# FFN down products two tiles behind, normed sums through PSUM, weight casts in other places: a two-block transformer kernel

## The chip, the cores and the metric

The kernel runs on one core of one Trainium2 chip. Its metric is the device time of one execution in microseconds. Five engines work side by side, each through its own queue in order: TensorE (PE, with its weight loads PEld), VectorE (DVE), ScalarE (ACT), GpSimd (POOL), and SyncE (SP), which here only issues DMAs. They wait for each other through semaphores.

## What is computed

The input is one sequence of 256 tokens of width 1024. Two transformer blocks follow each other. Cut to what matters:

```
first_block:  x = layer_norm(a*x + 0.5*swiglu(x))        # FFN0: silu(x@Wg) * (x@Wu) @ Wd, inner width 2816
              x = layer_norm(a*x + hybrid_mixer(x))      # q/k/v, three kinds of attention, gates, w_out
              x = layer_norm(a*x + 0.5*swiglu(x))        # FFN1
second_block: u = rmsnorm(h) @ w_in ...                  # convolution, gated delta rule, sparse attention
              h = h + rmsnorm(mixed @ w_o, w)            # normed sum 3
              f = causal_dwconv(rmsnorm(h) @ w_up) + b   # FFN2: three taps over the tokens
              h = h + rmsnorm((gelu(f_gate)*f_val) @ w_down, w)   # normed sum 4
              e = (p @ w_ple) * sigmoid(h @ w_ple_gate)
              h = h + rmsnorm(e, w)
```

All is float32. A product of float32 matrices is made of three TensorE passes over operands that are split into a high and a low part.

## The kernel before

**The stream.** All weights lie in one stream in the order of their use, as chunks of eight blocks of 128x128 (512 KB). SP loads chunk n into slot n % 4 of `ring`. ACT casts it to the high part (`high`, L1165, semaphore `hi_ready`), POOL subtracts for the low part in two instructions of 128x512 (L498, `lo_ready`), and TensorE takes both (`mm`, L529). When TensorE starts on a chunk it raises `used`; the cast of chunk n waits until chunk n-3 has been started, and stands in ACT's queue like all else, so what is behind it waits too. `feed_to` and `feed` (L1167 to L1177) issue the casts up to a given chunk; where they are called decides where the casts stand in ACT's order.

**An FFN** (`ffn`, L690) has 22 tiles of 128 hidden features. `gate_up_first` makes tiles 0 and 1 together from chunks 0 to 3, into `acc`, which is free then. `gate_up(f)` makes gate and up of tile f, 16 blocks (two chunks) and 48 matmuls of 256 columns, into a PSUM bank. ACT applies SiLU (`ffn_act`, L1183) and DVE multiplies and splits the result into `hT` (`hidden`, L1641; semaphores `h_made`, `hidden`). In FFN2 `geglu_act` (L1200) and `conv_hidden` do the same with a tap on ACT, four taps on DVE (L1672), GELU (L1213), product (L1680) and split. `down(f)` multiplies tile f by 8 blocks (one chunk, 12 matmuls of 512 columns) and adds into the four banks of `acc`. `down(0)` overwrites `acc`, so it waits for `h_made` of both first tiles. The order is: tiles 0 and 1, gate_up(2), down(0), down(1), gate_up(3), down(2), gate_up(4), down(3), and so on, gate_up(20), gate_up(21), and the last three down products in pieces (`HELD`). `ffn_end(f)` is the block up to which `feed` counts before ACT works on tile f. `hT` has four slots; `hidden(f)` waits until down(f-4) is done.

**Between the parts** there is a norm. For the layer norms `layer_half` (L1705) adds x and acc; `turn` transposes the normed tokens on TensorE (L651) into four PSUM banks, two of the eight xT tiles in each, ACT writes `xT_high` from them (L1255 to L1265) and DVE `xT_low` (L1848 to L1868). `layer_out` (L1734, L1735) then makes the residual from res and rows, a product and a sum of 128x1024 for each of two halves of the tokens (called tokens 0 and 1 below); it stands behind the q/k turn at once, and in FFN1 between the hidden tiles.

**Normed sums 3 and 4** (`add_normed`, L1787) stand before FFN2 and behind it. ACT squares each half row of `acc` (`acc_rms`, L1403) and takes the root (L1233); DVE multiplies acc by the norm's weights into `xs` (L1793, `acc_read`) and then multiplies by the reciprocal and adds the old x (L1797). Behind sum 3, ACT squares the sum again (`x_rms`) and copies the four `ple` banks (`ple_copy`, L1590), whose banks the turn before FFN2 writes. The last part, `into_acc`, is x @ w_ple_gate in eight steps of one chunk.

## Time and profile before

| what | value |
|---|---|
| median of three executions | 1193.85 us (1192.21 to 1196.79) |
| profiled execution | 1193.65 us, span 1191.8 us |
| mean granted TensorE clock | 0.976 |
| TensorE busy | 1114.9 us, 94% |
| POOL busy | 908.9 us, 76% |
| ACT busy | 628.6 us, 53% |
| DVE busy | 516.9 us, 43% |
| DMA | 193.40 MB, 162 GB/s |

The span runs from the first to the last instruction, and all times in the trace count from its start. FFN0 lies at 10 to 188 us, the q/k tiles at 200, FFN1 at 463 to 648, FFN2 at 963 to 1148, the last product at 1157 to 1180. A window's row gives its length, then the busy time of PE, PEld, DVE, ACT and POOL with the number of instructions in brackets, then the granted clock, the busy share of the DMA engines and GB/s. A timeline's row gives start, length, engine, line, operation, output <- inputs, size and count, and in brackets how long the engine had been idle and who released it. "issue" there means that the profile shows no releaser. Matmul ends are modelled; the distance between starts tells the pace. The granted clock has 1.00 for 2.4 GHz and 0.50 for 1.2 GHz.

### The profile page before, as it was taken

Reading aid. Unit: us, or ns where it says so; the run is one execution under the profiler, and the core shown is the slowest. Engines: PE = TensorE matmul, PEld = TensorE weight load, DVE = VectorE, ACT = ScalarE, POOL = GpSimd, SP = SyncE. Lnnn points to the kernel's source line nnn. Section 1 sums busy time; section 2 is a strip of 40 time slices with the busy share of each in tenths; the row PEclk is TensorE's granted clock in tenths of the full one; section 3 lists DMA queues with packets and bytes.
Section 4 is the critical chain, followed back from the end, with each engine's and each line's share of the span. In section 5 each row is a group of like instructions: output and inputs, shape, how many; then the busy total and the mean of one; then the engine's idle time right before and its main releaser. Section 6 shows DMA issues by size and latency. Waiting matters only on the chain.

```text
span 1191.8 us, 22559 instructions
## 1 busy us (share of the span) xinstructions
PE 1114.9 (94%) x8040; PEld 1034.4 (87%) x8040; DVE 516.9 (43%) x979; ACT 628.6 (53%) x1012; POOL 908.9 (76%) x700
## 2 busy tenths in 40 slices
PE   6999998899999998899998899899899989999986
PEld 6999998898988897799998889899788879999964
DVE  3333116232336544511113547774665245455664
ACT  4444446555556755344444765554556575555553
POOL 7999995998553595999998599393225869999973
PEclk9999999999998999999999899999989999999988
DMA  7866664576331364566565366252213655666641
GB/s 253 323 203 199 194 192 127 175 207 189 112 114 54 107 200 160 171 194 191 188 194 186 106 201 188 89 159 72 71 54 118 192 159 178 193 190 187 196 151 53
DMA packets 52631, 193.40 MB, mean 162 GB/s; under 512 B 5840, under 2 KB 6096, under 8 KB 51920
## 3 DMA queue, kind: packets, MB, share of 16 engines
q1 hardware_dynamic: 50976, 184.57, 49.8%
q10 hardware_dynamic: 1584, 7.81, 1.8%
q8 instruction: 53, 0.87, 0.3%
q14 instruction: 18, 0.15, 0.0%
HBM read 191.31 MB, written 1.05 MB: 161 GB/s over the span
## 4 chain that ended last, share of the span: by engine, by line
POOL 51%; issue 31%; PE 14%; DVE 2%; POOLq 1%; ACT 1%; DVEq 0%; ACTq 0%
POOL weights_low L498 51%; PE banks L529 8%; PE acc L529 6%; POOLq L501 0%; DVE xs L1797 0%; POOLq L495 0%; DVE stat L1812 0%; DVE res L1810 0%; DVE res L1824 0%; DVE act_buf L1672 0%; DVE xs L1830 0%; DVE xs L1793 0%; ACT weights_high L1165 0%; DVE hf L1680 0%; ACT act_buf L1208 0%
## 5 line engine op out<-in xcount | busy, mean ns | idle before, releaser
L498 POOL TENSOR_TENSOR weights_low<-ring,weights_high 128x512 fp32r<-128x512 f32 x696 | 908.7, 1336 | 263.9 <-ACT weights_high L1165 260.7
L1165 ACT CAST weights_high<-ring 128x1024 fp32r<-128x1024 f32 x348 | 361.5, 1048 | 242.8 <-PE banks L529 123.7
L529 PE MATMUL banks<-xT_high,weights_high 128*128 128x256 f32 x1536 | 432.0, 281 | 3.3 <-POOL weights_low L498 2.8
L529 PE MATMUL banks<-xT_low,weights_high 128*128 128x256 f32 x1536 | 427.4, 278 | 0.0
L529 PE MATMUL banks<-xT_high,weights_low 128*128 128x256 f32 x1536 | 427.2, 278 | 0.0
L529 PEld LDWEIGHTS banks<-xT_high,weights_high 128*128 128x128 f32 x1536 | 290.7, 189 | 7.2 <-issue 3.0
L529 PEld LDWEIGHTS banks<-xT_low,weights_high 128*128 128x128 f32 x1536 | 290.9, 189 | 2.3
L529 PEld LDWEIGHTS banks<-xT_high,weights_low 128*128 128x128 f32 x1536 | 290.3, 189 | 0.0
L1647 DVE TENSOR_TENSOR hf<-act_buf,banks 128x256 f32<-128x256 f32 x40 | 16.9, 421 | 247.4 <-ACT act_buf L1191 247.3
L529 PE MATMUL acc<-weights_high,hT_high 128*128 128x512 f32 x264 | 103.6, 392 | 7.6 <-issue 6.7
L529 PE MATMUL acc<-weights_low,hT_high 128*128 128x512 f32 x264 | 104.0, 394 | 0.0
L529 PE MATMUL acc<-weights_high,hT_low 128*128 128x512 f32 x264 | 103.0, 396 | 0.0
L529 PEld LDWEIGHTS acc<-weights_high,hT_high 128*128 128x128 f32 x264 | 50.0, 189 | 17.5 <-issue 7.7
L1672 DVE SCALAR_TENSOR_TENSOR act_buf<-banks,col,act_buf 128x255 f32<-128x255 f32 (+1 forms) x80 | 35.0, 478 | 58.9 <-ACT act_buf L1208 56.4
L529 PEld LDWEIGHTS acc<-weights_high,hT_low 128*128 128x128 f32 x264 | 49.9, 189 | 10.1
L1656 DVE TENSOR_TENSOR hT_low<-hf,hT_high 128x256 fp32r<-128x256 f32 x66 | 57.6, 873 | 2.3
L529 PEld LDWEIGHTS acc<-weights_low,hT_high 128*128 128x128 f32 x264 | 49.9, 189 | 9.2
L1279 ACT ACTIVATE prob<-sS,nmx 128x128 f32<-128x128 f32 x68 | 30.4, 448 | 48.1 <-DVE nmx L1886 47.9
L529 PE MATMUL acc<-xT_high,weights_high 128*128 128x256 f32 x144 | 39.0, 306 | 11.8 <-POOL weights_low L498 11.7
L1883 DVE SCALAR_TENSOR_TENSOR sS<-cst,banks 128x384 f32<-128x384 f32 x34 | 18.8, 554 | 64.5 <-issue 52.8
L1191 ACT ACTIVATE act_buf<-banks 128x256 f32<-128x256 f32 x40 | 15.4, 384 | 56.8 <-PE banks L529 56.8
L529 PEld LDWEIGHTS acc<-xT_high,weights_high 128*128 128x128 f32 x144 | 30.9, 214 | 12.2 <-issue 12.1
(337 smaller groups left out, 1620.6 us busy)
## 6 DMA issues: line engine op xcount, KB each, us to landing
ring<-in_stream SPq DMA_DIRECT2D x348, 512.0 KB, 3.6
rows<-in_big_rows ACTq DMA_DIRECT2D x3, 1024.0 KB, 6.9
rows<-in_big_rows ACTq DMA_DIRECT2D x3, 512.0 KB, 4.4
cst<-in_consts ACTq DMA_DIRECT2D x1, 1411.0 KB, 10.8
gates<-in_x_fm SPq DMA_DIRECT2D x2, 512.0 KB, 5.2
xs<-in_x_tm ACTq DMA_DIRECT2D x1, 1024.0 KB, 6.0
out<-xs SPq DMA_DIRECT2D x4, 256.0 KB, 2.1
pT<-in_p_fm ACTq DMA_DIRECT2D x1, 256.0 KB, 3.5
```

Source lines behind the costliest of these rows:

```text
L498: last = nc.gpsimd.tensor_tensor(wlo[:, slot, hs], ring[:, slot, hs], whi[:, slot, hs].bitcast(F32), ALU.subtract)
L529: ins = nc.tensor.matmul(o, lhsT, rhs, start=start, stop=stop, **kw)
L1165: nc.scalar.copy(whi[:, ch % RING, :], ring[:, ch % RING, :]).then_inc(S["hi_ready"], 1)
L1191: nc.scalar.activation(act_buf[:, f % 2, 0:T], ffn_tile(n, f, it)[:, 0:T], ACT.Silu).then_inc(S["act_done"], 1)
L1279: nc.scalar.activation(prob[:, j % 2, lo:hi], sS[:, j % 2, lo:hi], ACT.Exp, bias=nmx[:, j % 2, t:t + 1], accum_out=den[:, j % 2, t:t + 1]) ...
L1647: v.tensor_tensor(hf[:, f % 2, :], act_buf[:, f % 2, 0:T], ffn_tile(n, f, it)[:, T:2 * T], ALU.mult).then_inc(S["h_made"], 1)
L1656: v.tensor_tensor(hT[1][:, f % GROUP, :], hf[:, f % 2, :], hT[0][:, f % GROUP, :].bitcast(F32), ALU.subtract).then_inc(S["hidden"], 1)
L1672: last = v.scalar_tensor_tensor(buf, ffn_tile(2, f, it)[:, half * T:half * T + T - sh], conv_col(3 * (half * NF + f) + tap, it), buf, ALU. ...
L1883: mark(v.scalar_tensor_tensor(sS[:, j % 2, :], c("negdist"), slope, bank(f"s{j}")[:, 0:384], ALU.mult, ALU.add), "biased", j + 1)
```

## The change

The FFNs run two gate_up tiles ahead of the down products instead of one, and the stream is packed in that order: tiles 0 and 1, gate_up(2), gate_up(3), down(0), down(1), gate_up(4), down(2), gate_up(5), down(3) and so on to gate_up(20), down(18), gate_up(21), and the last three as before. `ffn_end` follows. ACT's `turn` casts the following part's fourth chunk between the xT tiles of its second and third bank. In `add_normed` the product with the weights stays in `acc`, the sum reads it from there, and DVE waits for each of its own instructions; TensorE's next use of `acc` waits for the sums (`norm_sum` 8, `xn_ready` 11) where it waited for the products (`acc_read` 16 and 20). Two casts around sum 3 and those of the last part stand behind squares that they stood before.

```
 def ffn_end(f):
-    return 32 if f < 2 else 24 * f + (8 if f < NF - 1 else 0)
+    return 32 if f < 2 else 16 * f + 16 if f < 4 else 24 * f
...
-            def into_acc(src, each, first_wait):
+            def into_acc(src, each, free):
...
-                        pe.wait_ge(S["acc_read"], first_wait)
+                        pe.wait_ge(S[free[0]], free[1])
...
-                    need(pe, "acc_read", 4 * n_acc_before)
+                    if first_acc:
+                        pe.wait_ge(S[first_acc[0]], first_acc[1])
...
-                    at[0] = b0 + (32 if f == 2 else 24 * f - 8 if f < NF - 1 else 24 * f - 16)
+                    at[0] = b0 + (16 * f if f < 4 else 24 * f - 16)
...
-                    at[0] = b0 + (48 if very_first else 24 * f + 32)
+                    at[0] = b0 + (64 + 8 * f if isinstance(it, int) and f < 2 else 24 * f + 48)
...
-                n_acc_before = (0, 2, 4)[n]
+                first_acc = (None, ("acc_read", 8), ("norm_sum", 8))[n]
                 gate_up_first()
                 gate_up(2)
+                gate_up(3)
                 down(0)
                 down(1)
-                for f in range(3, 1 + GROUP):
-                    gate_up(f)
-                    down(f - 1)
+                gate_up(4)
+                down(2)
                 with nc.tensor.Fori(1, (NF - 2) // GROUP - 1) as it:
                     for f in range(1, 1 + GROUP):
                         gate_up(f + GROUP, it - 1)
-                        down(f - 1 + GROUP, it - 1)
+                        down(f - 2 + GROUP, it - 1)
                 for f in range(NF - 1 - GROUP, NF - 1):
                     gate_up(f)
-                    if f < NF - 2:
-                        down(f - 1)
+                    down(f - 2)
                 gate_up(NF - 1)
...
-            into_acc(xT, (("xT_high", 32), ("xT_ready", 32)), 20)
+            into_acc(xT, (("xT_high", 32), ("xT_ready", 32)), ("xn_ready", 11))
...
-            def turn(i, gain=None, bias=None):
+            def turn(i, following, gain=None, bias=None):
                 for g in range(4):
+                    if g == 2:
+                        feed_to(PART_AT[following] // CB + 4)
...
             acc_rms(12, 0)
-            feed_to(PART_AT["ple"] // CB + 3)
+            feed_to(PART_AT["ple"] // CB + 2)
             acc_rms(12, 1)
             x_rms(4, 0, 0)
+            feed_to(PART_AT["ffn2"] // CB + 1)
...
             acc_rms(16, 0)
-            feed_to(PART_AT["ple_gate"] // CB + 1)
             acc_rms(16, 1)
-            feed_to(PART_AT["ple_gate"] // CB + 3)
-            turn(4)
+            feed_to(PART_AT["ple_gate"] // CB + 2)
+            turn(4, "ple_gate")
...
-                        mark(v.tensor_tensor(xs[:, dst, tok, hs], acc[:, 2 * tok + half, :], rows[:, i % 2, hs], ALU.mult),
-                             "acc_read", (12, 16)[i - 3] + 2 * tok + half + 1)
+                        link(v.tensor_tensor(acc[:, 2 * tok + half, :], acc[:, 2 * tok + half, :], rows[:, i % 2, hs], ALU.mult))
                     link(recip(stds + tok + 1, tok))
                     for half, (_, hs) in enumerate(halves(tok)):
-                        v.scalar_tensor_tensor(xs[:, dst, tok, hs], xs[:, dst, tok, hs], stat[:, 6 + tok:7 + tok], xs[:, src, tok, hs],
-                                               ALU.mult, ALU.add).then_inc(S[sem], 1)
+                        mark(v.scalar_tensor_tensor(xs[:, dst, tok, hs], acc[:, 2 * tok + half, :], stat[:, 6 + tok:7 + tok],
+                                                    xs[:, src, tok, hs], ALU.mult, ALU.add), sem, sem0 + 2 * tok + half + 1)
...
-    parts = [by_k(np.concatenate([g[0], u[0], g[1], u[1]]), 4), g[2], u[2], d[0], d[1]]
-    for f in range(3, NF):
-        parts += [g[f], u[f]] + ([d[f - 1]] if f < NF - 2 else [])
+    parts = [by_k(np.concatenate([g[0], u[0], g[1], u[1]]), 4), g[2], u[2], g[3], u[3], d[0], d[1]]
+    for f in range(4, NF):
+        parts += [g[f], u[f]] + ([d[f - 2]] if f < NF - 1 else [])
```

**Start of an FFN, TensorE.** FFN0, the end of gate_up(2) (banks<-xT) and what follows, first before and then after the change; the number ahead is the place in the queue.

```order
113 L529 MATMUL banks<-xT_high,weights_high 128x256
114 L529 MATMUL banks<-xT_low,weights_high 128x256
115 L529 MATMUL banks<-xT_high,weights_low 128x256
116 L529 MATMUL acc<-weights_high,hT_high 128x512
117 L529 MATMUL acc<-weights_low,hT_high 128x512
118 L529 MATMUL acc<-weights_high,hT_low 128x512
```

```order
113 L529 MATMUL banks<-xT_high,weights_high 128x256
114 L529 MATMUL banks<-xT_low,weights_high 128x256
115 L529 MATMUL banks<-xT_high,weights_low 128x256
116 L529 MATMUL banks<-xT_high,weights_high 128x256
117 L529 MATMUL banks<-xT_low,weights_high 128x256
118 L529 MATMUL banks<-xT_high,weights_low 128x256
```

Before, the down products (acc<-weights, hT) follow at place 116; after, 48 matmuls of gate_up(3) stand there first, and they follow at 164.

**Start of FFN2, ACT.** Taps of tiles 0 and 1 from acc (L1208), GELU (L1213), casts of chunks (L1165), then tile 2 from its bank; before and after.

```order
579 L1165 CAST weights_high<-ring 128x1024 x4
580 L1208 ACTIVATE act_buf<-acc,col 128x256 x2
581 L1213 ACT_TABLE_LOAD
582 L1213 ACTIVATE gel<-act_buf 128x256
583 L1208 ACTIVATE act_buf<-acc,col 128x256 x2
584 L1213 ACTIVATE gel<-act_buf 128x256
585 L1165 CAST weights_high<-ring 128x1024 x3
586 L1208 ACTIVATE act_buf<-banks,col 128x256 x2
587 L1213 ACTIVATE gel<-act_buf 128x256
588 L1165 CAST weights_high<-ring 128x1024 x3
```

```order
586 L1165 CAST weights_high<-ring 128x1024 x3
587 L1208 ACTIVATE act_buf<-acc,col 128x256 x2
588 L1213 ACT_TABLE_LOAD
589 L1213 ACTIVATE gel<-act_buf 128x256
590 L1208 ACTIVATE act_buf<-acc,col 128x256 x2
591 L1213 ACTIVATE gel<-act_buf 128x256
592 L1165 CAST weights_high<-ring 128x1024 x2
593 L1208 ACTIVATE act_buf<-banks,col 128x256 x2
594 L1213 ACTIVATE gel<-act_buf 128x256
595 L1165 CAST weights_high<-ring 128x1024 x2
```

The casts ahead of tile 0 are three instead of four, since one moved into the turn; behind the GELU of tile 1 stand two instead of three, and behind tile 2 two instead of three.

**Turn before the q/k tiles, ACT.** xT tiles from the banks, the bias part of each bank's second tile (tmp), casts, and the first q/k copies; before and after.

```order
75 L1259 ACTIVATE xT_high<-banks,col 128x256 x2
76 L1265 ACTIVATE tmp<-xT_high,col 128x256
77 L1259 ACTIVATE xT_high<-banks,col 128x256 x2
78 L1265 ACTIVATE tmp<-xT_high,col 128x256
79 L1259 ACTIVATE xT_high<-banks,col 128x256 x2
80 L1265 ACTIVATE tmp<-xT_high,col 128x256
81 L1165 CAST weights_high<-ring 128x1024 x3
82 L1328 ACTIVATE qkT<-acc 128x256 x3
```

```order
76 L1261 ACTIVATE xT_high<-banks,col 128x256 x2
77 L1267 ACTIVATE tmp<-xT_high,col 128x256
78 L1165 CAST weights_high<-ring 128x1024
79 L1261 ACTIVATE xT_high<-banks,col 128x256 x2
80 L1267 ACTIVATE tmp<-xT_high,col 128x256
81 L1261 ACTIVATE xT_high<-banks,col 128x256 x2
82 L1267 ACTIVATE tmp<-xT_high,col 128x256
83 L1165 CAST weights_high<-ring 128x1024 x2
84 L1330 ACTIVATE qkT<-acc 128x256 x3
```

One of the three casts behind the tiles now stands in their middle.

**Last norm, ACT.** Squares of acc (tmp, stat<-acc), small steps, the root (stat<-stat), casts, xT tiles; before and after.

```order
664 L1403 ACTIVATE tmp,stat<-acc 128x512
665 L1233 ACTIVATE stat<-stat 128x1
666 L1165 CAST weights_high<-ring 128x1024
667 L1403 ACTIVATE tmp,stat<-acc 128x512
668 L1407 ACTIVATE stat<-stat,cst 128x1
669 L1403 ACTIVATE tmp,stat<-acc 128x512
670 L1233 ACTIVATE stat<-stat 128x1
671 L1165 CAST weights_high<-ring 128x1024 x2
672 L1255 CAST xT_high<-banks 128x256 x8
673 L1165 CAST weights_high<-ring 128x1024 x5
```

```order
671 L1405 ACTIVATE tmp,stat<-acc 128x512
672 L1233 ACTIVATE stat<-stat 128x1
673 L1405 ACTIVATE tmp,stat<-acc 128x512
674 L1409 ACTIVATE stat<-stat,cst 128x1
675 L1405 ACTIVATE tmp,stat<-acc 128x512
676 L1233 ACTIVATE stat<-stat 128x1
677 L1165 CAST weights_high<-ring 128x1024 x2
678 L1257 CAST xT_high<-banks 128x256 x4
679 L1165 CAST weights_high<-ring 128x1024 x2
680 L1257 CAST xT_high<-banks 128x256 x4
681 L1165 CAST weights_high<-ring 128x1024 x4
```

The cast between the squares of the two tokens is gone; two casts stand ahead of the xT tiles and two among them.

## Rows read from the trace of the kernel before

**Rows 1.** Windows of the FFN bodies: length, busy us of each engine, TensorE's clock, DMA.

```profile
30.00:60.00 30.00, 30.00 (x208) 27.66 (x207) 9.98 (x13) 12.81 (x15) 27.87 (x22) 1.00 0.89 322
...
540.00:570.00 30.00, 30.00 (x217) 28.03 (x217) 4.57 (x12) 12.79 (x15) 28.08 (x22) 1.00 0.62 191
...
1050.00:1080.00 30.00, 30.00 (x217) 28.03 (x216) 15.52 (x26) 15.01 (x23) 28.71 (x23) 1.00 0.59 190
```

**Rows 2.** Chain of waits in FFN2: start, us, what.

```profile
1002.25 2.75 PE acc L529 x12
1005.00 5.47 PE banks L529 x48
```

**Rows 3.** Timeline of FFN1's start: start, us, what, [idle before <- releaser].

```profile
479.69 7.13 POOL L498 TENSOR_TENSOR weights_low<-ring,weights_high 128x512 fp32r<-128x512 f32 x4
...
481.21 2.28 DVE L1734 TENSOR_TENSOR xs<-res,rows 128x1024 f32<-128x1024 f32 x1
...
485.73 0.42 DVE L1647 TENSOR_TENSOR hf<-act_buf,acc 128x256 f32<-128x256 f32 x1
...
486.25 0.47 PE L529 MATMUL acc<-weights_high,hT_high 128*128 128x512 f32 x1 [4.63 <-issue]
...
486.81 1.05 ACT L1165 CAST weights_high<-ring 128x1024 fp32r<-128x1024 f32 x1 [6.42 <-PE acc L529]
...
498.88 0.39 PE L529 MATMUL acc<-weights_high,hT_high 128*128 128x512 f32 x1
```

**Rows 4.** Window behind the wait in FFN1, columns as in rows 1.

```profile
486.00:490.00 4.00, 3.75 (x10) 2.96 (x11) 3.90 (x5) 1.33 (x2) 2.88 (x3) 0.59 0.44 134
```

**Rows 5.** Timeline of the first q/k tiles, TensorE, POOL and DVE.

```profile
206.29 16.52 POOL L498 TENSOR_TENSOR weights_low<-ring,weights_high 128x512 fp32r<-128x512 f32 x10 [4.24 <-ACT weights_high L1165]
...
206.57 2.10 DVE L1734 TENSOR_TENSOR xs<-res,rows 128x1024 f32<-128x1024 f32 x1
...
209.94 0.36 PE L529 MATMUL banks<-xT_high,weights_high 128*128 128x256 f32 x1 [1.44 <-POOL weights_low L498]
...
214.39 0.36 PE L529 MATMUL banks<-xT_high,weights_high 128*128 128x256 f32 x1 [1.38 <-POOL weights_low L498]
```

**Rows 6.** Timeline of FFN2's start, ACT and TensorE.

```profile
981.68 2.93 ACT L1165 CAST weights_high<-ring 128x1024 fp32r<-128x1024 f32 x3
...
982.33 0.47 PE L529 MATMUL acc<-weights_high,hT_high 128*128 128x512 f32 x1 [2.05 <-issue]
...
985.58 0.47 PE L529 MATMUL acc<-weights_high,hT_high 128*128 128x512 f32 x1 [0.24 <-POOL weights_low L498]
```

**Rows 7.** Timeline of the turn before FFN1, ACT and TensorE.

```profile
468.52 2.01 ACT L1165 CAST weights_high<-ring 128x1024 fp32r<-128x1024 f32 x2
...
472.31 0.36 PE L529 MATMUL acc<-xT_high,weights_high 128*128 128x256 f32 x1 [1.47 <-POOL weights_low L498]
```

**Rows 8.** Timeline of FFN2's end, DVE and TensorE.

```profile
1142.52 1.57 DVE L1680 TENSOR_TENSOR hf<-gel,act_buf 128x256 f32<-128x256 f32 x1 [0.48 <-ACT gel L1213]
...
1144.56 0.47 PE L529 MATMUL acc<-weights_high,hT_high 128*128 128x512 f32 x1 [0.65 <-DVE hT_high L1654]
```

**Rows 9.** Two source lines of DVE: ns min/median/max, first and last start, forms.

```profile
L1797 DVE SCALAR_TENSOR_TENSOR xs<-xs,stat x8: 747/1093/1781, 949.7 to 1154.1; 128x512 f32<-128x512 f32 x8
...
L1705 DVE SCALAR_TENSOR_TENSOR res<-xs,acc x8: 686/687/690, 189.4 to 458.5; 128x512 f32<-128x512 f32 x8
```

**Rows 10.** Timeline of the last norm, ACT and DVE.

```profile
1148.02 1.03 ACT L1165 CAST weights_high<-ring 128x1024 fp32r<-128x1024 f32 x1
...
1152.80 3.03 DVE L1797 SCALAR_TENSOR_TENSOR xs<-xs,stat 128x512 f32<-128x512 f32 x2
```

**Rows 11.** Timeline of the norm before FFN2, ACT and TensorE.

```profile
950.19 2.00 ACT L1165 CAST weights_high<-ring 128x1024 fp32r<-128x1024 f32 x2 [1.14 <-PE acc L529]
...
959.06 1.05 ACT L1590 COPY gates<-banks 128x512 f32<-128x512 f32 x2
...
960.37 2.93 PE L651 MATMUL banks<-cst,res 128*128 128x128 f32 x16 [3.40 <-DVE res L1784]
```

More of the change, by code:

```diff
@@ L907, in _ @@
                 branch_b(n)
-            into_acc(mT1, (("merged_high", 0), ("merged", 0)), 4)
+            into_acc(mT1, (("merged_high", 0), ("merged", 0)), ("acc_read", 4))
             turn(1)
@@ L1124, in _ @@
                 done(mix_part(o, 1))
-            into_acc(mT2, (("merged_high", 8), ("mixed", 0)), 12)
+            into_acc(mT2, (("merged_high", 8), ("mixed", 0)), ("acc_read", 12))
             pe.wait_ge(S["p_split"], 1)
@@ L1319, in _ @@
             feed_to(PART_AT["qk"] // CB + 3)
-            turn(0, "ln_g0", "ln_b0")
+            turn(0, "qk", "ln_g0", "ln_b0")
             scale = {0: 0.125, 2: float(np.float32(32 ** -0.5)), 4: 0.125}
@@ L1392, in _ @@
             feed_to(PART_AT["ffn1"] // CB + 3)
-            turn(1, "ln_g1", "ln_b1")
+            turn(1, "ffn1", "ln_g1", "ln_b1")
             rows_in(2)
@@ L1450, in _ @@
             feed_to(PART_AT["conv"] // CB + 3)
-            turn(2, "mix_pre")
+            turn(2, "conv", "mix_pre")
             def conv_silu(t):
@@ L1602, in _ @@
             feed_to(PART_AT["ffn2"] // CB + 3)
-            turn(3, "ffn_pre")
+            turn(3, "ffn2", "ffn_pre")
             rows_in(5)
@@ L1785, in rms_scaled, with add_normed @@
                                     ).then_inc(S["xn_ready"], 1)
-            def add_normed(i, src, dst, sq, stds, sem):
+            def add_normed(i, src, dst, sq, stds, sem, sem0):
                 dve.wait_ge(S[f"big_rows_in{i % 2}"], 16 * (i // 2 + 1))
@@ L2260, in _ @@
             merged_low(mT2, 7, bank("mix7"), "mixed", 8)
-            add_normed(3, 1, 0, (4, 6), 8, "norm_sum")
+            add_normed(3, 1, 0, (4, 6), 8, "norm_sum", 4)
             rms_scaled(0, 10 + 1, 0)
@@ L2266, in _ @@
             steps[0] += NF
-            add_normed(4, 0, 1, (12, 14), 12, "xn_ready")
+            add_normed(4, 0, 1, (12, 14), 12, "xn_ready", 7)
             turn(4)
```

## The prediction

> **What bounds the kernel now.** I read the windows first, then the waits of TensorE, then the timeline around each wait. In the body of an FFN the reader is to see TensorE busy for 30.00 of 30 us, with POOL close behind at 28.08 (FFN1) and 28.71 (FFN2) [rows 1]; the chain of waits gives a tile's two halves, 2.75 us for a down product and 5.47 us for a gate/up pair, 8.22 us a tile [rows 2]. A tile uses three stream chunks, so **TensorE needs one chunk every 2.74 us whatever it computes from it**, and POOL makes one (two instructions of 28.08/22 = 1.28 us) in 2.55 us. Nothing that shifts work inside the loop can gain there: 66 tiles stay at 8.22 us. What can be won are the places where TensorE stands still, and the change touches six of them. I go by chunk number inside a part, from chunk 0, since the stream is repacked in the new order and chunk n is needed at the same distance before and after.
>
> **FFN1, first down product.** The first down product starts at 486.25 after 4.63 us of waiting [rows 3]. What it waits for stands above it: acc still holds tiles 0 and 1, and the product of tile 1 (DVE L1647) ends at 485.73 + 0.42, because DVE first multiplies token 0's rows of the layer norm (L1734, 2.28 us, and its partner). Then comes the price of the long stop: the granted clock is 0.59 from 486 to 490 [rows 4], the half level of 1.2 GHz for most of it. The third down product starts at 498.88 and is chunk 10; from 481.62, where the wait began and chunk 6 was due, four chunks at 2.74 us would reach it at 492.6. So 6.3 us stand between this and no stop. After the change gate_up(3) fills 5.47 us, to 487.1, and h_made is there at 486.2: the wait is gone. Next late is POOL. It made chunks 7 and 8 from 479.69 to 486.82, 3.56 us each beside DVE's products [rows 3], and then lay idle; now it goes on, and DVE's rows of token 1 meet it. At 3.5 us a chunk, chunk 11 is ready at 486.82 + 3 x 3.5 = 497.3 against a need at 495.3: 2.0 us are lost again, and 0.2 for restarts. **Term: 4.1 us**, bounds 1.6 (4.4 us a chunk, as between TensorE's two late starts in [rows 5]) and 6.3. The row is nearest to 3.5, since DVE also has casts and waits between.
>
> ACT's order has to allow it. Its casts for tile 2 stop at block 48 instead of 56, so the SiLU of tile 2 no longer stands behind a cast that waits 6.42 us for the first down product [rows 3]. The same bound 24f holds later, with the same distance to the end of gate_up(f) as 24f + 8 had: no effect per tile.
>
> **FFN2, first down product.** Here the wait is 2.05 us [rows 6], with no lowered clock. But the second down product, chunk 7, waited too, for POOL, till 985.58; its cast is the first of the three at 981.68, behind both GELUs. That cast does not move: ACT finishes GELU of tile 1 in both orders before it. Now chunk 7 is the second half of gate_up(3), due at 983.0, and stands till 985.5 as before. One wait takes the other's place. **Term: 0.1 us**, bounds -0.3 and 2.2.
>
> **FFN0** has no wait there: from 30 to 60 us TensorE is busy 30.00 of 30 us, at 322 GB/s [rows 1]. ACT now issues the norm's 1 MB table after the SiLU of tile 3 without waiting for three casts, some 5 us earlier, while the start's tables still load. At 322 GB/s 1 MB is 3.3 us of the queues; the ring holds four chunks, 11 us. Term 0, bounds -1 and 0.
>
> **A cast between xT tiles.** In the turn before FFN1 chunk 3 is cast at 468.52, when all eight tiles are done, and TensorE waits 1.47 us for its low part [rows 7]. After tile 3 the cast starts at about 465.6, and the low part is ready before TensorE's need at 470.8. Tiles 4 to 7 come 1.05 us later; tile 4 is then there at 467.2 and is first used at 468. **Term: 1.5 us**, bounds 0.4 (if that 1.05 shows) and 1.6. In the turn before the q/k tiles TensorE waits 1.44 and 1.38 us, and POOL works 16.52 us on five chunks [rows 5], slowed by DVE's row products from 206.57 on. With chunk 3 out of the way before these begin, chunk 4 is in time (211), but chunk 5 is made wholly beside them and is late by 1.4 us, where the two waits made 2.8. **Term: 1.4 us**, bounds 0.5 and 2.8. Before the convolution and before FFN2 no such wait exists; the tiles that slip by 1.05 us are needed more than 2 us later: 0. Before the last product the cast of chunk 3 waits till TensorE has begun chunk 0 with xT tile 0; it stands before tiles 4 to 7 only, due 11 us later: 0.
>
> **End of FFN2.** The last tile's hidden product took 1.57 us beside POOL, and the last held unit waited 0.65 us for its cast [rows 8]. Before, gate_up(20) and gate_up(21) stood in a row; now a down product parts them, ACT's casts come sooner, and POOL is done earlier. **Term: 0.7 us**, bounds 0 and 0.8.
>
> **Normed sums through PSUM.** L1797 reads xs twice from SBUF and takes 0.747 to 1.781 us; L1705, the same operation and size with one input in acc, takes 0.686 to 0.690 [rows 9]. After the change the sum has one input in acc. In the last norm the pair for token 1 takes 3.03 us and ends at 1155.83, which releases the last transposes [rows 10]. Two at 0.69 save 1.6. The cast of 1.03 us that stood between the squares of tokens 0 and 1 moves behind them: 0.9 of it arrives, as DVE's rest becomes shorter too. Some 0.4 goes back since the transposes of the first half now end later than the second half's data. The in-place product is priced as L1705 too; the added waits of DVE for its own sums queue nothing but the next sum. The last product now waits for the sums instead of the first products, but xT waits for these sums anyway: 0. **Term: 2.1 us**, bounds 1.0 and 2.6. In the norm before FFN2 the transposes at 960.37 start just when ACT ends its copies of the ple banks (959.06 + 1.05) [rows 11], since they write those banks. ACT does the same work between 950.19 and that point, in another order, without a pause: two casts, six squares, four copies. **Term: 0**, bounds -0.3 and 1.
>
> Against this stands a table of the Trainium skill ("VectorE: DVE Perf Modes", section "The TRN2 errata — SBUF-src ops pay a fixed extra latency per instruction"): a VectorE instruction from PSUM costs 120 cycles plus its length, one from SBUF 58. By it each sum and each product through acc would be some 0.06 us slower, and an estimate from the page is 0.3 us lost in each norm, in place of 2.1 won. The rows say otherwise (0.69 through acc, 0.75 at best without), and I go by them.
>
> **Sum.** 4.1 + 0.1 + 0 + 1.5 + 1.4 + 0.7 + 2.1 + 0 = 9.9 us. The profiled execution took 1193.65 us (span 1191.8), 0.2 below the median of 1193.85: 1193.65 - 9.9 = 1183.75, **1183.8 us**.
>
> **Rivals.**
> - *POOL eats the gain.* Wherever DVE reads two operands from SBUF, both crawl; POOL takes 4.4 us a chunk, as [rows 5] show at their worst. FFN1 gives 1.6, q/k 0.5: 9.9 - 3.4 = 6.5, **1187 us**. For: both waits that go are followed by DVE's row products. Against: 3.56 us a chunk in [rows 3]. The Trainium skill ("SBUF — State Buffer", section "Who interferes with whom") has a VectorE instruction with two SBUF inputs contend with GpSimd, and one with one input not; the same rule backs the term of the norms.
> - *All waits go.* FFN1 6.3, FFN2 2.2, q/k 2.8, norms 2.6: 9.9 + 2.2 + 2.1 + 1.4 + 0.5 = 16.1, **1177.5 us**. Against: chunk 7 in [rows 6].
> - *The starts don't change.* ACT's casts, in order behind SiLU and GELU, hold the chunks back as at 981.68, so that FFN1 gives nothing and q/k 0.5; 9.9 - 4.1 - 0.9 = 4.9 us are left, **1189 us**.
> - *Slower: POOL becomes the pace of the FFN loops.* POOL has 8.22 x (1 - 28.71/30) = 0.35 us to spare per tile in FFN2 and 0.53 in FFN1. With down two tiles behind, the split of a hidden tile falls beside other casts; if contention adds 0.8 us to POOL's tile, TensorE waits 0.27 us in each of 44 tiles and 0.45 in 22, 22 us, less the 10: **1206 us**. It decides from 0.35 us a tile on. Against: casts, SiLU and splits keep their distance to the gate_up that they follow, and POOL never pauses enough for a new overlap.
>
> **Chances.** Forecast 0.64, POOL eats 0.14, all go 0.08, starts unchanged 0.09, slower 0.05. The bounds of the terms add to 1.9 and 17.3, so 1176 to 1192; these ends need every term at its edge. The range of 1178.5 to 1188.5 holds the forecast, the first rival and half of the second. A measurement of this kernel can tell about 0.5% (6 us) from no change. Faster by more: the forecast, the second rival and half of the first, 0.79; within: 0.16; slower: 0.05.
>
> **What would show it.** Right: no wait before the first down product of FFN1 and no lowered clock behind it; waits for POOL of about 0.5 to 1 us there instead; in FFN2 a wait of 2.4 us in the middle of gate_up(3); no wait for chunk 3 in the turn before FFN1; sums of 0.69 us; tiles at 8.22 us. The forecast is wrong if the tiles' period moves, if the clock drops at a place where it was full, or if the waits for POOL in FFN1 add to over 4 us.

## Result and profile after

The changed kernel took 1188.8 us (median of ten executions, 1181.3 to 1192.8); the kernel before, timed beside it, 1196.19 us (ten executions, 1191.6 to 1201.9). The ratio is 0.9928 [0.9901, 0.9954]: 0.7% faster, 5.5 to 11.8 us, where 9.9 was forecast. The median itself lies 0.3 us above the range, because the kernel before stood 2.3 us higher in this comparison than the 1193.85 from which the forecast counted.

The two profiled executions differ by much less: 1191.8 before, 1191.0 after. The profile after is of the slowest of its ten executions. So the question is twofold: did the terms arrive, and what took 7 to 10 us back in this one execution? The first rows are TensorE's starts around the first down product of FFN1, with DVE, ACT and POOL (they answer [rows 3]).

```profile
479.27 11.09 POOL L498 TENSOR_TENSOR weights_low<-ring,weights_high 128x512 fp32r<-128x512 f32 x7
...
483.37 2.31 DVE L1736 TENSOR_TENSOR xs<-res,rows 128x1024 f32<-128x1024 f32 x1
...
490.50 0.47 PE L529 MATMUL acc<-weights_high,hT_high 128*128 128x512 f32 x1 [0.46 <-POOL weights_low L498]
...
494.16 0.47 PE L529 MATMUL acc<-weights_high,hT_high 128*128 128x512 f32 x1 [0.65 <-POOL weights_low L498]
...
497.69 0.35 PE L529 MATMUL banks<-xT_high,weights_high 128*128 128x256 f32 x1 [0.52 <-POOL weights_low L498]
...
503.41 0.40 PE L529 MATMUL acc<-weights_high,hT_high 128*128 128x512 f32 x1
...
511.83 0.40 PE L529 MATMUL acc<-weights_high,hT_high 128*128 128x512 f32 x1
```

The wait of 4.63 us is gone, and three waits for POOL of 1.6 us in all stand there, beside DVE's row products. The clock stays up where [rows 4] had 0.59. This is the window around and behind the first of these waits, columns as in [rows 1]:

```profile
490.00:494.00 4.00, 3.06 (x13) 2.17 (x12) 3.96 (x3) 1.38 (x2) 4.00 (x4) 1.00 0.46 133
```

But the last two rows above are two down products in a row, and 8.42 us lie between them, not 8.21. TensorE waits for nothing there. The chain of waits in FFN2 of the same execution still has the pieces of [rows 2]:

```profile
1050.90 2.75 PE acc L529 x12
1053.64 5.47 PE banks L529 x48
```

The second thing that was not there before is in the timeline behind the q/k tiles, DVE, POOL and TensorE:

```profile
234.97 38.98 POOL L498 TENSOR_TENSOR weights_low<-ring,weights_high 128x512 fp32r<-128x512 f32 x31
...
238.53 35.44 DVE L1935 TENSOR_TENSOR stat<-stat 128x1 f32<-128x1 f32 x1 [22.10 <-ACT stat L1328]
...
274.19 1.95 DVE L1940 COPY v<-banks 128x384 f32<-128x384 f32 x4
...
275.31 0.66 PE L529 MATMUL banks<-weights_high,xT_high 128*128 128x384 f32 x1 [6.40 <-DVE v L1940]
```

**A subtraction of one element per partition takes 35.44 us.** It ends at 273.97, when POOL's row of instructions ends (234.97 + 38.98 = 273.95; the 31 shown are the end of that row, and 29 of them run beside the subtraction). The copies of v stand behind it on DVE, and TensorE waits 6.40 us for the first. In the profile before, the same instruction (L1934) took 7.81 us and hid.

Third, FFN2's start and the sums (they answer [rows 6], [rows 8], [rows 9] and [rows 10]): a timeline, a source line's ns, and the timeline again.

```profile
987.20 0.39 PE L529 MATMUL banks<-xT_high,weights_high 128*128 128x256 f32 x1 [2.07 <-POOL weights_low L498]
...
1146.46 0.47 PE L529 MATMUL acc<-weights_high,hT_high 128*128 128x512 f32 x1 [0.41 <-DVE hT_high L1656]
```

```profile
L1798 DVE SCALAR_TENSOR_TENSOR xs<-acc,stat,xs x8: 750/751/753, 950.1 to 1154.8; 128x512 f32<-128x512 f32 x8
```

```profile
1153.96 1.54 DVE L1798 SCALAR_TENSOR_TENSOR xs<-acc,stat,xs 128x512 f32<-128x512 f32 x2
```

To read the terms in spite of what comes by chance, I cut TensorE's work at starts that both orders have. Each number is the time between two such starts in the trace, us; "turn" is the first transpose of a turn, "held" the first of the last held down products of an FFN, "attention" the first matmul of q and k. f_ kernels come below.

| stretch | before | after | f_before | f_norms_casts | f_order | f_after |
|---|---|---|---|---|---|---|
| start to q/k turn | 196.2 | 195.3 | 195.0 | 195.1 | 195.1 | 196.2 |
| q/k turn to attention | 85.1 | 91.6 | 85.2 | 84.4 | 86.0 | 84.5 |
| attention to FFN1's turn | 178.2 | 177.3 | 176.8 | 177.6 | 176.6 | 176.1 |
| FFN1's turn to held | 184.5 | 182.4 | 189.4 | 182.2 | 183.6 | 180.3 |
| held to next turn | 14.4 | 14.4 | 14.4 | 14.4 | 14.4 | 14.4 |
| that turn to FFN2's turn | 302.0 | 299.8 | 301.1 | 302.5 | 298.5 | 300.0 |
| FFN2's turn to held | 178.6 | 180.4 | 177.3 | 178.9 | 183.0 | 178.9 |
| held to last turn | 10.8 | 10.5 | 10.8 | 10.7 | 10.2 | 10.5 |
| last turn to TensorE's end | 30.3 | 27.5 | 29.8 | 29.0 | 30.5 | 27.8 |

### The profile page after: what moved, and what is told of

Same layout as the page of the kernel before. It is cut to its first block, busy times and chain, and to the rows that moved or that the text cites. A ratio compares the mean times of both kernels' runs of the same rounds, so it can differ in the third digit from the quotient of the medians.

```text
span 1191.0 us, 22555 instructions
## 1 busy us (share of the span) xinstructions
PE 1117.0 (94%) x8040; PEld 1038.5 (87%) x8040; DVE 554.1 (47%) x979; ACT 627.8 (53%) x1012; POOL 908.4 (76%) x700
## 3 DMA queue, kind: packets, MB, share of 16 engines
q10 hardware_dynamic: 1584, 7.81, 1.8%
## 4 chain that ended last, share of the span: by engine, by line
POOL 52%; issue 31%; PE 14%; DVE 2%; POOLq 1%; ACT 0%; DVEq 0%; ACTq 0%
POOL weights_low L498 52%; PE banks L529 8%; PE acc L529 6%; POOLq L501 0%; POOLq L495 0%; DVE stat L1813 0%; DVE res L1825 0%; DVE res L1811 0%; DVE xs L1798 0%; DVE xs L1831 0%; DVE acc L1795 0%; PE banks L651 0%; DVE act_buf L1674 0%; ACT tmp L1405 0%; DVE hf L1682 0%
## 5 line engine op out<-in xcount | busy, mean ns | idle before, releaser
L1165 ACT CAST weights_high<-ring 128x1024 fp32r<-128x1024 f32 x348 | 361.4, 1048 | 239.1 <-PE banks L529 129.6
L1658 DVE TENSOR_TENSOR hT_low<-hf,hT_high 128x256 fp32r<-128x256 f32 x66 | 66.3, 1004 | 2.3
L529 PEld LDWEIGHTS acc<-weights_high,hT_high 128*128 128x128 f32 x264 | 49.6, 188 | 11.2 <-issue 1.7
L529 PEld LDWEIGHTS acc<-weights_high,hT_low 128*128 128x128 f32 x264 | 49.6, 188 | 10.5
L1935 DVE TENSOR_TENSOR stat<-stat 128x1 f32<-128x1 f32 x1 | 35.4, 35436 | 22.1 <-ACT stat L1328 22.1
```

Of the source, the lines that this page charges most:

```text
L529: ins = nc.tensor.matmul(o, lhsT, rhs, start=start, stop=stop, **kw)
L1165: nc.scalar.copy(whi[:, ch % RING, :], ring[:, ch % RING, :]).then_inc(S["hi_ready"], 1)
L1658: v.tensor_tensor(hT[1][:, f % GROUP, :], hf[:, f % 2, :], hT[0][:, f % GROUP, :].bitcast(F32), ALU.subtract).then_inc(S["hidden"], 1)
L1935: link(v.tensor_tensor(stat[:, 60:61], stat[:, 19:20], stat[:, 18:19], ALU.subtract))
```

## Experiments

**1 to 4: the one-element instructions rewritten, and the change in two halves.** The first theory on the 35.44 us is that this subtraction has two SBUF inputs, and that such a DVE instruction can wait as long as POOL works without a pause. So it, and the four one-element products of the layer norms, were written with one tensor and a scalar column:

```diff
-link(v.tensor_tensor(stat[:, 60:61], stat[:, 19:20], stat[:, 18:19], ALU.subtract))
+link(v.tensor_scalar(stat[:, 60:61], stat[:, 19:20], stat[:, 18:19], None, ALU.subtract))
...
-mark(v.scalar_tensor_tensor(stat[:, 58 + tok:59 + tok], stat[:, 12 + 2 * tok:13 + 2 * tok], -1.0, stat[:, 6 + tok:7 + tok],
+mark(v.tensor_scalar(stat[:, 58 + tok:59 + tok], stat[:, 12 + 2 * tok:13 + 2 * tok], -1.0, stat[:, 6 + tok:7 + tok],
```

Four kernels have this: the one before (f_before), the changed one (f_after), the one before with only the new order of down products, stream and bounds (f_order), and with all but that (f_norms_casts).

> The kernel before, with the one-element subtraction behind the q/k tiles (L1934) and the four one-element products of the layer norms (L1714) written with one SBUF tensor and a scalar column in place of two SBUF tensors. Theory A (in the profile of the changed kernel that subtraction stood 35.44 us beside POOL's unbroken row of instructions and ended when POOL paused, 273.95 us; in the profile before it took 7.81 us and hid; so it is two SBUF inputs against POOL): the subtraction takes 0.25 us or less, and the time is that of before or a few us less (1190 to 1196), since before lost something only in executions in which it stood over 20 us. Rival B (any DVE instruction on SBUF waits there, not the kind with two inputs): the subtraction still takes 5 to 40 us and nothing changes.

> The changed kernel with the same one-element instructions rewritten. Theory A: the subtraction takes 0.25 us or less, TensorE's wait of 6.40 us for the copies of v is gone, and the median falls from 1188.8 to 1183 to 1187. Rival B: the wait stays and so does the time. On FFN1: theory C (the slow tiles of 8.42 us in place of 8.21 belong to down products two tiles behind): FFN1 is at 8.42 again. Rival D (they are a state of TensorE that an execution falls into at a stop): FFN1 may be at 8.21 here, and another part at the slower rate of 118 ns per matmul of 256 columns in place of 114.

> The kernel before with the rewritten one-element instructions and of the change only the new order of the down products (stream, bounds of ACT's casts, order of TensorE). By the terms of the prediction it gains 4.1 + 0.1 + 0.7 = 4.9 us against f_before. Theory C (tiles of 8.42 us in FFN1 come with the order): only 4.9 - 3.6 = 1.3 us, and FFN1's tiles at 8.42. Rival D (a state of TensorE that comes by chance): FFN1's tiles at 8.21 or 8.42 and a gain near 4 to 5 us in the median. No wait before FFN1's first down product either way.

> The kernel before with the rewritten one-element instructions and all of the change but the order of the down products: sums through PSUM, casts between xT tiles and behind the squares. By the terms of the prediction it gains 1.5 + 1.4 + 2.1 = 5.0 us against f_before (bounds 1.9 to 7.0). Theory C: tiles of 8.21 us everywhere. Rival D: one of the three FFNs may show 8.42 here too. If the two parts don't depend on each other, the gains of f_order and of this one add up to that of f_after over f_before.

Measured: f_before 1193.63 us, ratio to before 0.9992 [0.9966, 1.0017]; f_order 1187.53, 0.9935 [0.9912, 0.9958]; f_norms_casts 1185.77, 0.9919 [0.9886, 0.9953]; f_after 1182.47, 0.9901 [0.9873, 0.9930]. The source line of the subtraction in f_after, and its neighbour of the layer norm:

```profile
L1935 DVE TENSOR_SCALAR stat<-stat x1: 214/214/214, 239.6 to 239.6; 128x1 f32<-128x1 f32 x1
...
L1716 DVE TENSOR_SCALAR stat<-stat x4: 214/214/215, 195.0 to 458.1; 128x1 f32<-128x1 f32 x4
```

214 ns in place of 7.8 and 35.4 us, beside the same POOL: rival B falls. Of the four products of the layer norms one took 1.00 us ahead of the q/k turn and one ahead of FFN1's turn (L1716 in the changed kernel: 158 to 1001 ns); each takes 0.21 now. In all four f_ kernels the 11.0 us from FFN0's held products to the q/k turn are 10.2.

The halves gain 6.1 and 7.9 us on f_before, together 14.0; both at once gain 11.2. With executions of one kernel 10 us apart, this neither shows nor excludes that they overlap; both are there, each about as large as forecast or more (4.9 and 5.0).

**Theory C falls here**: the slow tiles don't belong to the new order. f_before has the old order, and all tiles of its FFN1 lie 8.42 us apart, those of the kernel before 8.21; f_after has the new order, and its FFN1 and FFN2 run at 8.21. f_order has the slow tiles in FFN1 and FFN2: its FFN2 gives, in the chain of waits,

```profile
1053.23 2.77 PE acc L529 x12
1056.00 5.66 PE banks L529 x48
```

That is 118 ns from one matmul of 256 columns to the next, in place of 114, at a granted clock of 1.00 and with no wait in it.

**5: stops on purpose.** Is it a stop that decides the rate? In f_after TensorE was made to wait once in each round of the loops:

```diff
 gate_up(f + GROUP, it - 1)
+if f == 2:
+    pe.wait_ge(S["hidden"], NF * n + f + GROUP + 1 + GROUP * (it - 1))
 down(f - 2 + GROUP, it - 1)
```

> f_after, with TensorE made to wait in every round of the FFN loops (four tiles) for the hidden tile it has just projected, about 1.2 to 1.5 us; 4 stops in each of the three FFNs, 12 in all, so 14 to 18 us slower. Rival D (a stop decides at which of two rates, 114 or 118 ns per matmul of 256 columns, TensorE goes on): the rate changes at some of these stops, also inside an FFN. Theory E (the rate is set by something else, the time, the part of the program or the chip's warmth): each FFN runs at one rate throughout, as in every trace so far.

Measured: 1231.9 us (one execution), 49 slower, not 14 to 18. The loops run three rounds, so there are nine stops, not twelve, and they take 2.0 to 5.7 us each, not 1.2 to 1.5, some with a stretch at the half clock behind. At the stop ahead of 602.20, SiLU, product and split take 1.7 us with no cast between them (ACT starts at 600.27, DVE ends at 601.98); in FFN2, where taps and GELU belong to the chain, the stops take 5.4 to 5.7. The run still shows what it was made for. Down products of FFN1, TensorE's timeline:

```profile
583.47 0.39 PE L529 MATMUL acc<-weights_high,hT_high 128*128 128x512 f32 x1
...
591.69 0.39 PE L529 MATMUL acc<-weights_high,hT_high 128*128 128x512 f32 x1
...
602.20 0.50 PE L529 MATMUL acc<-weights_high,hT_high 128*128 128x512 f32 x1 [2.14 <-DVE hT_low L1660]
...
610.71 0.40 PE L529 MATMUL acc<-weights_high,hT_high 128*128 128x512 f32 x1
...
619.13 0.40 PE L529 MATMUL acc<-weights_high,hT_high 128*128 128x512 f32 x1
```

8.22 us a tile ahead of the stop at 600.1, 8.42 behind it. At four of the nine stops the rate changes, twice to the slow one and twice back; inside an FFN's body, between the stops, it doesn't change. Theory E falls, and rival D stands as far as that a stop can change the rate. It isn't the only thing that can: in FFN0 of f_after the rate is 114 ns to 39 us, 118 from 40 to 48 and 114 behind that, with no wait that the profile lists. At the first of these two changes one matmul starts about 0.1 us late (39.46 us), at the second none does. What sets it is open. In the thirteen other traces the rate is slow through 7 of 39 FFN bodies, 2 of 15 in kernels with the old order and 5 of 24 with the new; a body at the slow rate costs 18 to 20 times 0.20, about 4 us.

**6 to 8: what is left at the starts.** In FFN2, as the prediction had it, chunk 7 is late behind both GELUs. g_chunk7 casts it ahead of ACT's work on tile 1; g_rows_later moves DVE's row products in FFN1 behind tiles 2 and 3; g_both has both. All are made on f_after.

```diff
-feed(PART_AT["ffn2"] + ffn_end(f), it)
+feed(PART_AT["ffn2"] + (40 if isinstance(f, int) and f == 1 else ffn_end(f)), it)
...
-if f < 2:
-    layer_out(1, 0, f)
+if f in (2, 3):
+    layer_out(1, 0, f - 2)
```

> f_after, with ACT's cast of chunk 7 of FFN2 placed before its two copies of tile 1 instead of behind the GELU of tile 1. Theory A (FFN2's first stop is that of chunk 7, whose cast stands behind both GELUs): the wait of 2.07 to 2.42 us for POOL in the middle of gate_up(3) goes, and with it the stretch at the half clock of 1.3 us that followed it in f_after; the stretch from the transposes before FFN2 to the first down product falls from 27.9 to 24.2 to 25.5 us, the time by 2.4 to 3.7 us against f_after. Rival B (POOL is late anyway, for its later chunks): waits of 2 us stand a few us later and nothing is won.

> f_after, with DVE's row products of the layer norm before FFN1 (four of 128x1024) behind the hidden tiles 2 and 3 of FFN1 instead of 0 and 1. Theory A (these products, with two SBUF inputs, slow POOL to 3.5 us or more a chunk just where it has no lead): the waits for POOL between 488 and 498 us (0.5 to 1.6 in all) go or come 6 us later, smaller; a gain of 0 to 1.5 us. Rival B (POOL is short of lead there for want of casts, not for DVE): the waits stay where they are.

> f_after with both edits, chunk 7's cast earlier and the row products later. If the two are what remains of the waits at the FFNs' starts and do not disturb each other: 1178 to 1180 against f_after's 1182.5. If POOL is late anyway: 1182.

Measured: g_chunk7 1179.84 us, 0.9897 [0.9853, 0.9941]; g_rows_later 1182.59, 0.9890 [0.9850, 0.9929]; g_both 1179.84, 0.9885 [0.9857, 0.9914]. With g_chunk7 the wait of 2.42 is gone, and the stretch from FFN2's turn to the first down product falls from 27.9 to 25.9. Then POOL is late twice more, by 0.55 and 1.11, and up to the eighth down product 80.4 us become 79.4. So it is between theory A and rival B: about 1 us of 2.4 to 3.7. g_rows_later only moves the waits: in f_after one of 0.53 at 491.9, here 0.59 at 493.0 and 0.55 at 496.6. Rival B stands, nothing is won. g_both and g_chunk7 have the same median, the lowest of all kernels here, 14.7 us ahead of before's 1194.52, so moving the rows adds nothing to the cast; that either beats f_after the intervals don't show.

The stretch behind FFN2's wait shows where the new order loses time. TensorE's windows of f_after, with its clock in the third column from the right:

```profile
973.00:975.00 2.00, 0.00 (x0) 1.00 0.00 0
975.00:977.00 2.00, 1.61 (x13) 0.97 0.38 45
977.00:979.00 2.00, 2.00 (x12) 0.50 0.57 219
979.00:981.00 2.00, 2.00 (x9) 0.68 0.86 254
```

After a wait of 2.42 us the clock falls to the lower level of 1.2 GHz for some 3 us, and the 24 matmuls behind the wait take 4.03 us, where 24 at 114 ns take 2.73. In five of the six kernels with the new order and this wait (g_stops not counted) it falls there, and these 24 matmuls take 4.0 to 4.5 us; in the sixth, the changed kernel itself, it doesn't, and they take 2.85. Of the five kernels with the old order, whose wait of 1.8 to 2.05 us is followed by a down product, only one shows it (h_norms, below).

**9 to 10: the subtraction put back.** f_after and f_before again with the subtraction as a tensor_tensor, the four products still rewritten.

> f_after with one instruction put back: the one-element subtraction behind the q/k tiles again with two SBUF inputs. Theory A (it is this instruction that costs the changed kernel its 6 us against f_after, since it stands until POOL pauses, and in the new order POOL doesn't pause before the copies of v are due): it stands 25 to 36 us again, ends where POOL's row of instructions has a pause, TensorE waits 4 to 7 us for v, and the median is 1186 to 1189. Rival B (35.44 us was one unlucky execution): it stands under 15 us, hidden, and the median is within 2 us of 1182.5.

> f_before with the same instruction put back. In the profile before it stood 7.81 us. If the new order matters for it, it stands under 20 us here and hides: 1192 to 1195, as f_before. If it is chance alone, any length up to 36 us, and over some 25 us a wait of TensorE for v.

Measured: k_sub_after 1183.49 us, 0.9904 [0.9869, 0.9939]; k_sub_before 1196.52, 1.0015 [0.9986, 1.0045]. The subtraction and POOL beside it in k_sub_after:

```profile
232.88 19.10 POOL L498 TENSOR_TENSOR weights_low<-ring,weights_high 128x512 fp32r<-128x512 f32 x15
...
239.79 6.96 DVE L1935 TENSOR_TENSOR stat<-stat 128x1 f32<-128x1 f32 x1 [22.94 <-ACT stat L1328]
```

6.96 us here and 9.60 in k_sub_before, both hidden. **My theory A falls, rival B stands**: as far as these two traces and medians show, 35.44 us was one execution's bad luck, and not the 6 us that part the medians of the changed kernel and f_after. The subtraction doesn't need a long pause of POOL either: here it ends at 246.76, in the middle of POOL's row. Each of the four lengths seen (6.96, 7.81, 9.60, 35.44) ends where one POOL instruction ends and the next hasn't begun. At most such places inside POOL's rows the next record begins 0.03 to 0.06 us before the last one ends; where the subtraction ended, a gap stands there instead, of 0.02 to 0.06 us in three kernels and of 3.2 in the changed one. Not every gap serves: k_sub_before passed one of 0.03 us and the changed kernel three of 0.05. Why is not shown. Of the 6 us, some 1.6 are the two products of 1.00 us ahead of the turns (0.79 each); the rest lies inside the intervals.

**11 to 12: the sums alone, and all but the sums.** h_norms is f_before with only the sums through PSUM; h_casts_order is f_after with the sums as before.

```diff
-mark(v.tensor_tensor(xs[:, dst, tok, hs], acc[:, 2 * tok + half, :], rows[:, i % 2, hs], ALU.mult), ...
+link(v.tensor_tensor(acc[:, 2 * tok + half, :], acc[:, 2 * tok + half, :], rows[:, i % 2, hs], ALU.mult))
...
-v.scalar_tensor_tensor(xs[:, dst, tok, hs], xs[:, dst, tok, hs], stat[:, 6 + tok:7 + tok], xs[:, src, tok, hs],
+mark(v.scalar_tensor_tensor(xs[:, dst, tok, hs], acc[:, 2 * tok + half, :], stat[:, 6 + tok:7 + tok],
```

> f_before with only the sums through PSUM, casts and order as before. The prediction's term for the last norm was 2.1 us: 1.6 from the two sums of token 1 at 0.69 in place of 3.03 (0.75 in the profile of the changed kernel, so 1.5), and 0.9 less 0.4 from the cast moved behind the squares. From the first transposes of the last norm to TensorE's last matmul (29.8 us in f_before, 27.8 in f_after): theory A 28.2 to 28.6. Rival (the cast made the wait, the sums were only late with it): 29.5 or more.

> f_after with the sums through SBUF as in the kernel before, all else changed. Theory A: the same stretch takes 29.0 to 29.5 us (27.8 plus 1.5 for the sums), the sums of token 1 of the last norm take over 1 us each beside POOL. Rival (the moved cast made the gain): 28.0 or less. The time is 1184 under A and 1182.5 under the rival.

Measured: h_norms 1191.43 us, 0.9976 [0.9947, 1.0006]; h_casts_order 1183.96, 0.9897 [0.9842, 0.9951]. The times are too close; the stretch is not. From the last turn to TensorE's end h_norms takes 27.8 us against 29.8 in f_before, h_casts_order 29.2 against 27.8 in f_after. The pair of sums of token 1 beside POOL, in h_norms and in h_casts_order (DVE's timeline):

```profile
1149.25 1.54 DVE L1797 SCALAR_TENSOR_TENSOR xs<-acc,stat,xs 128x512 f32<-128x512 f32 x2
```

```profile
1146.17 2.78 DVE L1798 SCALAR_TENSOR_TENSOR xs<-xs,stat 128x512 f32<-128x512 f32 x2
```

Both pairs differ in the clock as well, however. TensorE's windows over this turn, first of h_norms, then of f_before:

```profile
1148.00:1164.00 16.00, 14.20 (x61) 0.89 0.42 132
```

```profile
1150.00:1166.00 16.00, 12.66 (x53) 0.79 0.42 132
```

Of the traces with as long a stay at the lower clock as f_before's, the five with the sums through PSUM take 28.6 to 29.1 us, the five without 29.2 to 30.5. The pair f_norms_casts and f_before parts by 0.8. TensorE's waits inside this turn, behind its first transpose, depend less on chance. They are 1.8 us in all nine traces with the sums through PSUM, h_norms with its old casts among them; 3.3 to 3.8 in the four with old sums and old casts; and in h_casts_order:

```profile
1147.34 1.12 PE L651 MATMUL banks<-cst,xs 128*128 128x128 f32 x4 [2.01 <-DVE xs L1798]
...
1149.01 1.12 PE L651 MATMUL banks<-cst,xs 128*128 128x128 f32 x4 [0.56 <-DVE xs L1798]
```

So the sums through PSUM by themselves take 1.5 to 2.0 us of waiting away, of which some 1 us reaches the end at an equal clock. The moved cast takes 0.8 to 1.2 away where the sums go through SBUF, and nothing more where they go through PSUM.

## Why the prediction was right, and where it was not

- **What bounds the loops.** A chunk per 2.74 us held wherever TensorE ran at its usual rate. That the tiles' period could move by 2.5% with no wait was not in the prediction, which took a moved period for a sign of POOL. POOL is not it: from 540 to 570 us in f_before's slow FFN1 it is busy for 27.41 us, less than in [rows 1].
- **FFN1's start, 4.1, and its turn, 1.5.** FFN1's stretch from turn to held fell by 2.1 us in the changed kernel, which had 18 slow tiles (3.6 us; 5.7 without). Where no tile was slow the new order and the cast in the turn gained, against before's 184.5: 4.2 (f_after, whose turn was at the lower clock for 6.8 us, before's for 3.4), 5.2 (k_sub_after), 5.5 (h_casts_order), 5.6 (g_chunk7). 5.6 was forecast. In detail: no wait for `h_made`, no lowered clock, 1.6 us of waits for POOL in place of the 2.0 forecast, and POOL at 3.2 us a chunk (11.09/3.5), not 3.5. The chunk-3 wait of 1.47 us is gone.
- **q/k turn, 1.4.** One wait of 1.38 us is left, as forecast. The stretch gained 0.7 us from f_before to f_norms_casts, inside the bounds of 0.5 to 2.8. The changed kernel lost 6.5 there: the subtraction (6.40), which no row of before warned of except by its 7.8 us for one element.
- **FFN2's start, 0.1: the step that failed.** The place was right, the wait stands in the middle of gate_up(3) at 2.07 to 2.42 us for the forecast 2.4. Its price was not: the step took "no lowered clock" over from [rows 6] to a place with other work around it. The 24 matmuls behind it lose 1.3 us in f_after. In the changed kernel itself the clock stayed up there. FFN2's stretch was 1.8 us longer than before in the changed kernel and 1.6 longer in f_after than in f_before; in the changed kernel it was a longer stay at the lower clock in the turn instead (0.50 and 0.55 over 6 us, for 0.63 and 0.80 before). How far down and how long a turn goes differs from execution to execution: f_before and f_after show 1.00 throughout FFN2's turn. So the 1.8 us of the changed kernel arose in the turn and not at this step, and f_norms_casts, in the old order, has the same 178.9 us as f_after.
- **End of FFN2, 0.7.** 0.2 to 0.3 arrived wherever FFN2 ran at its usual rate. The 0.6 of f_order are no gain of the change: in it, as in g_rows_later and h_casts_order, FFN2 ran at the slow rate, and the hidden product was there before TensorE came for it. The wait fell from 0.65 to 0.41 only, since the product beside POOL still takes 1.38 us.
- **Last norm, 2.1.** 2.8 us in the changed kernel, 2.0 in f_after and in h_norms, but 0.8 in f_norms_casts, with the clock as in f_before. The prediction's sum counted 1.6 for the sums and 0.9 less 0.4 for the cast; the runs show the sums' part, and behind it nothing of the cast's. The sums take 0.751 us, not 0.69: L1705 has a constant factor where this line has a scalar column, so the row to take was the least of L1797 itself, 0.747. The Trainium skill ("VectorE: DVE Perf Modes", "The TRN2 errata — SBUF-src ops pay a fixed extra latency per instruction") would by an estimate from its table make each sum 0.06 us slower through PSUM. The rows don't agree: 0.751 stands against 0.744 at best through SBUF. The prediction counted the products in this as well, but they read `acc` in both kernels. The Trainium skill has the rule that a VectorE instruction with at most one SBUF input, outside the modes that use two ports, doesn't contend with GpSimd ("SBUF — State Buffer", "Who interferes with whom"). Every sum through PSUM (0.749 to 0.753) and the rewritten one-element instructions (0.214) agree with it.
- **FFN0, 0; norm before FFN2, 0.** Both held in the changed kernel: 184.3 us to FFN0's held products as against 185.2, and the wait ahead of FFN2's turn 3.42 as against 3.40. FFN0 isn't free in every execution: f_after has 186.0, for 184.8 in f_before, with a wait of 0.89 for POOL at 57.25, behind a cast that had waited 5.54 us for its chunk's DMA. The term's lower bound of -1 allows for about this much.
- **The rivals.** "POOL becomes the pace" fell as a mechanism. "POOL eats the gain", "all waits go" and "starts unchanged" are refuted by FFN1's rows.
- **The sum, and luck.** By the stretches, FFN1 gives 4.2 to 5.6 us (with its turn), q/k 0.7, the end of FFN2 0.2 to 0.3 and the last norm 0.8 to 2.0, while FFN2's start costs 0 to 1.3 and FFN0 0 to 1.2. That makes 3.4 to 8.6 us, less than the 9.9 forecast. The 7.4 between the medians of the first comparison lie inside this, and their interval, 5.5 to 11.8, holds the forecast too. The medians of f_before and f_after part by 11.2, more than these terms explain; that is open. So the path of the prediction is shown, but that its sum comes within a few us of the measured gain is in part luck.

## What to carry to other kernels

When a stop is moved, its length moves with it, but its price (the lowered clock behind it) has to be priced anew at the new place. When executions of a kernel differ by 1%, cut the trace at starts that both versions have, look first at the distance of matmul starts and at the clock behind each stop, and only then at the change. A DVE instruction with two SBUF inputs may be as small as one element and still stand for 35 us beside a busy POOL: give it a scalar column or a PSUM input, above all where TensorE's operands stand behind it.

## What the runs showed of the hardware

- TensorE has two rates for the same stream of 256-column matmuls at a granted clock of 1.00, 114 and 118 ns a start (tiles of 8.21 and 8.42 us), constant through an FFN's body in thirteen traces; 4 of 9 stops put into the bodies changed it. Unexplained.
- A one-element DVE instruction with two SBUF inputs took 6.96, 7.81, 9.60 and 35.44 us beside back-to-back POOL instructions, the same with a scalar column 0.214. It ended each time at a gap between two POOL records, of 0.02 to 0.06 us in three cases and 3.2 in the longest.
- The same stop of about 2 us brought a stretch at the lower clock in some kernels and none in others, and a turn ran at clocks from 1.00 down to 0.50 in the same place.
